# A two-block model on one core: the second layer's modulation sums moved from the first block into the first recurrent layer, and six fixed experts in a new order of units

## The reference

```python
merged = jax.nn.sigmoid(ga) * y_a + jax.nn.sigmoid(gb) * y_b
x = x + merged @ w_out[l]
h2 = rms_norm(x, norm2_g[l]).reshape(B * T, D)
# top-1 group of 4, top-2 of its 8 experts: 256 tokens, 2 of 32 experts each
for e in range(N_EXPERTS):
    he = jax.nn.silu(h @ w_gate[e]) * (h @ w_up[e])
    y = y + comb[:, e:e + 1] * (he @ w_down[e])
x = x + y
```

```python
c_act = jax.nn.silu(c)
for l in range(DEPTH_2):
    mod = c_act @ w_ada[l] + b_ada[l]          # (1, 3072), w_ada[l] is 1024 x 3072
    shift, scale, gate = jnp.split(mod, 3, axis=-1)
    h = rms_norm_2(x, norm_g[l]) * (1.0 + scale[:, None, :]) + shift[:, None, :]
    u = h @ w_in[l]
    rg_x, rg_z, ml_x, ml_o, ml_z = jnp.split(u, split_pts, axis=-1)
    ... # y_rg: conv of 4 taps, gates, linear recurrence; y_ml: conv, q, k, v, chunked mLSTM
    y = jnp.concatenate([y_rg, y_ml], axis=-1) @ w_out[l]
    x = x + gate[:, None, :] * y
```

## Time and profile before

| | |
|---|---|
| median of 3 runs | 1090.07 us (1086.15 to 1094.87) |
| the profiled execution | 1092.46 us, span 1090.70 us |
| mean granted TensorE clock | 0.952 |
| busy: PE, DVE, ACT, POOL | 990.6, 418.7, 262.2, 166.7 us |
| TensorE's first pass on an expert, last mix | 302.31; ends 524.8 us |
| layer 0: from the first transpose | 541.61 us |
| layer 1: from the first transpose | 812.09 us |
| read from memory | 224.76 MB, 207 GB/s over the span |

### The profile page before, as it was taken

The page is one execution under the profiler, slowest core; times in us unless marked ns, Lnnn a source line. Parts: engine busy times, 40 slices in busy tenths (PEclk is TensorE's granted clock), DMA queues, the critical chain, the costliest instruction groups (busy, mean ns, idle before and its releaser), DMA issues.

```text
span 1090.7 us, 14384 instructions
## 1 busy us (share of the span) xinstructions
PE 990.6 (91%) x5605; PEld 784.5 (72%) x5605; DVE 418.7 (38%) x922; ACT 262.2 (24%) x597; POOL 166.7 (15%) x147
## 2 busy tenths in 40 slices
PE   4979999999899999776499999999989999999995
PEld 4857877788766555443288887887868888788784
DVE  2149762247613131111552470634235246163411
ACT  2122222201311212100308143223011714323200
POOL 5477997601100000000000000000000000000000
PEclk9888999989899999888799999999999999999998
DMA  8774866449999999999534443323433444332301
GB/s 237 251 252 130 244 215 209 155 149 302 398 376 420 421 420 421 420 422 407 166 116 155 154 154 118 116 78 100 132 116 125 146 154 154 117 117 78 116 1 58
DMA packets 138448, 226.79 MB, mean 208 GB/s; under 512 B 6329, under 2 KB 124434, under 8 KB 126090
## 3 DMA queue, kind: packets, MB, share of 16 engines
q1 hardware_dynamic: 136632, 221.41, 56.9%
q0 software_dynamic: 1600, 4.35, 1.6%
q10 hardware_dynamic: 146, 0.08, 0.0%
HBM read 224.76 MB, written 1.06 MB: 207 GB/s over the span
## 4 chain that ended last, share of the span: by engine, by line
PE 77%; SPq 7%; DVE 6%; DMA 4%; ACT 3%; issue 2%; DVEq 0%; ACTq 0%; POOLq 0%
PE bank L456 32%; PE bank L1039 10%; SPq L1076 7%; PE bank L902 5%; PE bank L767 4%; PE bank L673 3%; PE bank L917 3%; DMA s<-in_w_up 3%; PE bank L743 2%; PE bank L803 2%; PE bank L782 2%; PE bank L439 1%; DMA ring<-in_w_in 1%; PE bank L566 1%; PE bank L932 1%
## 5 line engine op out<-in xcount | busy, mean ns | idle before, releaser
L456 PE MATMUL bank<-hT,ring 128*128 128x256 f32 x1488 | 332.9, 383 | 0.0
L456 PEld LDWEIGHTS bank<-hT,ring 128*128 128x128 f32 x1488 | 282.3, 192 | 44.5 <-issue 7.1
L1039 PE MATMUL bank<-ring,s 128*128 128x256 f32 x512 | 114.4, 386 | 3.3 <-DVE s L1923 3.3
L1039 PEld LDWEIGHTS bank<-ring,s 128*128 128x128 f32 x512 | 99.2, 194 | 17.8 <-DVE s L1923 3.8
L2063 POOL DMA_DIRECT2D gateB<-in_final_g x1 | 0.6, 594 | 545.9 <-DVE x L1931 545.9
L767 PE MATMUL bank<-s,z 128*32 128x256 f32 (+1 forms) x448 | 64.6, 432 | 9.0 <-DMA s<-in_w_up 5.8
L1720 DVE SCALAR_TENSOR_TENSOR z<-z,bank 128x256 f32<-128x256 f32 x10 | 4.2, 421 | 162.2 <-ACT z L1276 161.1
L2016 POOL TENSOR_TENSOR ring<-ring,csil 128x2048 f32<-128x2048 f32 x17 | 61.3, 3604 | 18.1 <-PE bank L482 17.2
L902 PE MATMUL bank<-ring,hT 128*128 128x256 f32 x256 | 56.1, 380 | 0.0
L902 PEld LDWEIGHTS bank<-ring,hT 128*128 128x128 f32 x256 | 48.5, 190 | 7.4 <-issue 0.9
L767 PEld LDWEIGHTS bank<-s,z 128*32 128x32 f32 (+1 forms) x448 | 35.2, 133 | 19.4 <-issue 15.3
(11 more groups left out here) (387 smaller groups left out, 1431.5 us busy)
## 6 DMA issues: line engine op xcount, KB each, us to landing
ring<-in_w_in SPq DMA_DIRECT2D x56, 1024.0 KB, 5.1
ring<-in_w_ada SPq DMA_DIRECT2D x24, 1024.0 KB, 6.0
ring<-in_w_out SPq DMA_DIRECT2D x20, 1024.0 KB, 5.0
s<-in_w_down SPq DMA_DIRECT2D x18, 1024.0 KB, 20.0
s<-in_w_gate SPq DMA_DIRECT2D x15, 1024.0 KB, 25.4
s<-in_w_up SPq DMA_DIRECT2D x13, 1024.0 KB, 21.5
ring<-in_w_up SPq DMA_DIRECT2D x12, 1024.0 KB, 20.8
ring<-in_w_gate SPq DMA_DIRECT2D x10, 1024.0 KB, 21.9
```

The lines of the kernel that those rows point to most:

```text
L456: mm = pe.matmul(b[:, 0:T], w[:, (k0 + kb) * CW + m * P:(k0 + kb) * CW + (m + 1) * P], rhs[:, kb, :], start=(kb == 0), stop=(kb == nk - 1))
L1039: mm = pe.matmul(xo[j, tt][:, 0:CW], yT[:, kb, tt * P:(tt + 1) * P], w[:, kb, :], start=(kh == 0 and kb == 0), stop=(kh == 1 and kb == KB ...
```

## The change

1. The 12 chunks of layer 1's modulation leave the first block. They stand between layer 0's weight chunks: one after each of rx and rz, after every second mx, and after each of the first two chunks of the output gate. GpSimd sums all 24; VectorE's sums are gone. The second twelve go to a new tile `adasum1` with two buffers, so GpSimd starts chunk n when TensorE has used n - 2. GpSimd starts on them behind its pads, which wait for the norm at the head of layer 0. In the first block, eight chunks stand as before and four beside ga.
2. Six experts are fixed (0 to 5), so 18 parts can be loaded before the routing is known, as many as there are slots. Two places are left for heavy ones.
3. The sequence is SLSLSLHLLL. The parts of the three fixed pairs are loaded first, then all others in order of use; each part beyond the 18th takes the slot of the part used 18 places before it.
4. The product that sorts the keys (`reorder_out`) stands between the gates and the ups of unit 0 instead of behind both, and VectorE's picks for unit 1 stand behind its result.
5. The branch without slots walks over units instead of pairs, with four buffers of activations.

```diff
-FIXED, HEAVY, LIGHT_SLOTS = 4, 4, 32
-SEQUENCE = "SSLHLLHLLL"
+FIXED, HEAVY, LIGHT_SLOTS = 6, 2, 32
+SEQUENCE = "SLSLSLHLLL"
...
-ADA_CHUNKS = LAYERS * 3 * D // CW
+ADA_CHUNKS = 3 * D // CW
 ADA_LAG = 2
-ADA_POOL = 17
...
+        adasum1 = sb("adasum1", [P, 2, CW])
...
         for c in (C_GA, C_GB):
             for j in range(4):
                 add((full, cols_of(w_in, c + j * CW)))
-                add_ada()
+                if c == C_GA:
+                    add_ada()
...
+        def addt_ada():
+
+            l, j = ada_left.pop(0)
+            tail_ada.append(len(tail))
+            addt((full, cols_of(a["w_ada_2"][l], j * CW)))
         for l in range(LAYERS):
             wi2 = a["w_in_2"][l]
             for j in range(4):
                 addt((full, cols_of(wi2, j * CW)))
+                if l == 0:
+                    addt_ada()
...
+        expert_use = [(j, c) for _, j0, G in UNITS for c in range(3) for j in range(j0, j0 + G)]
+        expert_order = [(j, c) for j, c in expert_use if LOAD_RANKS[j] < FIXED] + \
+            [(j, c) for j, c in expert_use if LOAD_RANKS[j] >= FIXED]
+        expert_chunk = {jc: E0 + m for m, jc in enumerate(expert_order)}
+        slot = [n % RING for n in range(NB1)] + moe_slots
+        for m in range(NM, 3 * EXPERTS):
+            before = expert_chunk[expert_use[m - NM]]
+            assert before < E0 + m
+            slot.append(slot[before])
+        slot += [(NB1 + t) % RING for t in range(len(tail))]
...
+                    if (u, c) == (0, 0):
+                        reorder_out()
...
                         for m in range(2):
                             projT(w, m, hT, A, f"{name}{l}{2 * j + m}")
                         used()
+                        if l == 0 and (name == "rz" or j % 2):
+                            ada_job()
...
-                out_gate(0)
-                out_gate(1)
+                for j in range(2):
+                    out_gate(j)
+                    if l == 0:
+                        ada_job()
...
                 headT(wq, lambda k: mc[:, k, :], "mq")
                 used()
+                if l == 0:
+                    for _ in range(ADA_LAG):
+                        ada_sum()
...
+                    c = ada_at[n]
+                    g.wait_ge(slot_full[slot[c]], fill_value[c])
+                    back = 3 if n < ADA_CHUNKS else 2
+                    if n >= back and not ADA_CHUNKS <= n < ADA_CHUNKS + back:
+                        g.wait_ge(A.done, A.upto(f"ada{n - back}"))
...
             step(g.memset(vaug[:, :, :, MLD:VW], 1.0), S["pads_ready"])
+            ada_sums(ADA_CHUNKS)
             g.wait_ge(S["layer_done"], LAYERS)
```

More of the change, by code:

```diff
@@ L339, in build @@
         ada_chunks = []
-        ada_left = [(l, j) for l in range(LAYERS) for j in range(3 * D // CW)]
+        ada_left = [(l, j) for l in range(LAYERS) for j in range(ADA_CHUNKS)]
         def add_ada(n=1):
@@ L389, in build @@
                 addt((full, cols_of(a["w_out_2"][l][kh * D:(kh + 1) * D, :], j * CW)))
+        assert not ada_left
         E0 = NB1
@@ L680, in _ @@
                     route(j - 1, (0, 1), (A.free, A.upto(f"xT{j - 1}1")))
-                for _ in range((1, 1, 2, 0)[j]):
-                    ada_job()
             turn_x(A, 3, (0,))
@@ L686, in _ @@
             route(3, (1,), (C.free, C.upto("xT31")))
-            for _ in range(ADA_LAG):
-                ada_job()
             pe.wait_ge(S["routed"], 1)
@@ L859, in _ @@
                 pe.wait_ge(S["xgT_ready"], 4)
-                for p in range(PAIRS):
-                    pair_all(p)
+                for u in range(NU):
+                    unit_all(u)
             for j, c in expert_order:
@@ L1101, in _ @@
                         sp.wait_ge(*sem_value)
-                if j >= FIXED and j not in ids:
+                if LOAD_RANKS[j] >= FIXED and j not in ids:
                     if not ids:
@@ L1227, in _ @@
                     step(f(oaT[o:o + 64, g // 2, :], b[o:o + 64, 0:T], ACT.Copy), A.free)
-            for _ in range(4):
-                ada_job()
             load_root_table()
@@ L1321, in _ @@
                     out_copy(rxv[:, m, PAD:PAD + T], T)
+                    if l == 0 and m % 2:
+                        ada_job()
                 for h in range(KB):
@@ L1342, in _ @@
                     out_copy(mxv[:, m, PAD:PAD + T], T)
+                    if l == 0 and m in (3, 7):
+                        ada_job()
                 act.wait_ge(S["rg_root_wanted"], l + 1)
@@ L1559, in _ @@
                 step(tten(gmT[:, g, :], b[:, 0:T], guT[:, g, :], ALU.mult), B.free)
-            ada = {"n": ADA_POOL}
-            def ada_sums(count):
-                for n in range(ada["n"], ada["n"] + count):
-                    c = ada_chunks[n]
-                    v.wait_ge(slot_full[c % RING], fill_value[c])
-                    v.wait_ge(A.done, A.upto(f"ada{n - 3}"))
-                    w, dst = full(ring[c % RING]), adasum[:, n % 3, :]
-                    step(tsc(dst, w[:, 0, :], csil[:, 0:1], None, ALU.mult))
-                    for kb in range(1, KB):
-                        ins = stt(dst, w[:, kb, :], csil[:, kb:kb + 1], dst, ALU.mult, ALU.add)
-                        step(ins, S["ada_summed_v"]) if kb == KB - 1 else step(ins)
-                ada["n"] += count
             v.wait_ge(S["small_loaded"], 16 * 5)
@@ L2009, in ada_sums @@
                 for n in range(ada["n"], ada["n"] + count):
-                    c = ada_chunks[n]
-                    g.wait_ge(slot_full[c % RING], fill_value[c])
-                    if n >= 3:
-                        g.wait_ge(A.done, A.upto(f"ada{n - 3}"))
-                    w = full(ring[c % RING])
+                    c = ada_at[n]
[3 more added lines that the diff above has]
+                        g.wait_ge(A.done, A.upto(f"ada{n - back}"))
+                    w = full(slots_of[slot[c]])
                     step(g.tensor_tensor(w, w, csil[:, :].unsqueeze(2).broadcast_to([P, KB, CW]), ALU.mult))
```

157 lines of the change are left out of this document (80 added, 77 removed).

## The result

| | before | after |
|---|---|---|
| median | 1089.48 us (1086.15 to 1094.87, 4 runs) | 1127.45 us (1124.22 to 1129.36, 4 runs) |
| span of the profiled execution | 1090.7 us | 1125.3 us |
| mean granted TensorE clock | 0.952 | 0.943 |
| busy: PE, DVE, ACT, POOL | 990.6, 418.7, 262.2, 166.7 us | 997.0, 454.2, 262.5, 234.1 us |

The account below looks back on a forecast made before the run. It took transfers to bound the experts' stage and TensorE the first block and layers. Saving 3.4 us before layer 0 and losing 29.7 in it gave +26.3: 1116 us, own range 1108 to 1124, 8 in 10 1100 to 1129.

Parts of the forecast that it names:

- rival 3: Layer 0 costs its upper bound of 38 us and starving takes all the prefetch's gain: 1128; chance 0.12.
- (b): Layer 0's first convolution: VectorE held by GpSimd, gate products 5 us later, then a 1.4 us bank wait.
- (c): Layer 0's second convolution, held by GpSimd: output gate's fourth tile waits 6.1 us, chunk 24's sum 2.5 before k.
- the clock: TensorE's granted clock in layer 0, partly at its lower level behind the waits: 1.4 us more.
- What bounds the kernel: Whole kernel: experts' stage bound by transfers, first block and the two layers by TensorE.
- First block and experts' stage: Before layer 0: earlier order, 18 parts loaded ahead, then unit 1 starved of slots; 3.4 us less in all.
- (a): Layer 0's head: VectorE's chain held at each GpSimd instruction, so TensorE starts 9.0 us late.
- block 7 ends at about 670: Second convolution's last block, delayed by GpSimd: end at about 670 us where it was 638.9.
- The weighed rule: Skill's rule: GpSimd contends only with two-port or two-SBUF-input VectorE instructions; (b) and (c) would be about 2 us less.
- Rival 1: Layer 0: VectorE not slowed where it matters, layer 0 costs only 7.1 us, total 1094; chance 0.10.
- Rival 2: Experts' stage: prefetch pays, DMA never starves, gain 17 us instead of 3.4, total 1103; chance 0.12.
- Rival 4: Experts' routing: the change does not do what it says, all goes through the dense branch, over 1200; chance 0.01.

Follow-up runs that it names:

- late_pairs: Changed kernel with sequence SSLSLLHLLL, GpSimd waiting for the normed x and, after two of layer 1's chunks, for the first convolution; 1113.64 us.
- late_head: Changed kernel with one more wait: GpSimd starts layer 1's chunks only when the normed x is ready; 1116.38 us.
- split_sums: Changed kernel with layer 1's chunks summed in eight GpSimd instructions of at most 512 columns instead of four; 1112.91 us.
- fine_sums: Changed kernel with layer 1's chunks summed in pieces of 256 columns, 15 GpSimd instructions a chunk; 1130.24 us.

## Why the prediction was right or wrong

The measured 1127.45 lies outside the forecast's own range (1108 to 1124) and inside the range of 8 in 10 only because that one reaches to rival 3, so the hit is a narrow one. On the profiled execution 1118.8 was said and 1127.0 measured, 8.2 us more. Of these, layer 0 up to k has 8.1 (37.8 for 29.7), nearly all in (b), (c) and the clock.

**What bounds the kernel** held: the experts' stage on transfers, layer 0 on TensorE until VectorE is late. One row was misread: the 27.36 us of the earlier trace rows are a w_up load from issue to landing, and TensorE's wait for it, at 505.87, is 6.16.

**First block and experts' stage: -3.4 said, -4.8 measured.** The course was as told: unit 0's gates at 299.56 (said 298.9), the fourth up in unit 1 at 329.85 (said 329.2), the pass ending at 335.53 (said 335.5). Only the wait is 7.58 and not 9. The prediction's own end times, 518.1 and 521.5 from starts 3.4 us apart, leave nothing for the prefetch; the traces show 2.75 for the start and 2.05 for the stage itself, so the near hit is in part luck. The starving behind the filled slots was the right reason for the small gain: the 277 GB/s are the same in late_pairs with another order. Not foreseen: 1.15 us between the last mix and L893. VectorE's last sum ends 0.8 us behind the mix in both kernels (520.76, 525.55); what grew is its idle time behind that, 5.22 us for 4.07, for which the profile names no releaser. The cause is open.

**(a) The head: 9.0 said, 9.1 measured.** The chain of holds, worked out instruction by instruction from four rows of the first block, gave TensorE's delay to 0.1 us, and late_head confirms the cause.

**(b) The first convolution: 5.0 + 0.7 said, 7.5 measured.** The blocks end at one per chunk, as told. Not in the sum: the gate products behind the wait (4.32 us, at 590.05) run at TensorE's lower clock (0.54 granted over 590.05 to 593.68), 1.22 us for two matmuls that take 0.67 elsewhere. Up to rz they take 593.68 - 590.05 = 3.6 us, where the kernel before had 2.0: 1.6 of the 1.8 us that were missing. The bank wait behind it is 1.29, said 1.4.

**(c) The output gate: 6.1 said, 10.92 measured. This is the term that was mis-sized.** The step that failed is "block 7 ends at about 670". That is in the times of before. The changed kernel comes to layer 0 3.65 us sooner (L893 at 527.52 for 531.17), so it stands for 666.4 in its trace, and the block ended at 674.30, 7.9 us later. TensorE came to the fourth tile 3.1 us later than in the sum (664.35 for 671.0 - 6.1 - 3.65 = 661.25), and the difference, 4.8, is what the wait has too much. I had said that three blocks (2, 6, 7) cross GpSimd's work, and let GpSimd run at 8.26 us a chunk. In the trace the wide instructions of the gates (L1845 to L1847, L1850) are held, 2.29 becoming 4.29 in the first and 3.95 in the last; the convolution so starts at 629.35, behind them, and not at 612.74 as before; and GpSimd is held in turn, with its instruction of 1.27 at 3.19 and that of 3.60 at 5.53, so that a chunk there takes up to 12 us, and its later chunks lie over more of the convolution. Five blocks of eight were held, and four of them took over 8 us. The 1.4 us for the clock was too little as well: the gate products lost 1.6, the pass behind this wait 1.7, and the k projection's pass, behind the end of the sum, another 1.7. The wait for chunk 24's sum was right, 2.19 for 2.5.

**The weighed rule.** The prediction took the convolution's first instruction, "one input at 0.41 us for 256 columns", for one that the rule would let go free. It was held, to 3.68 us at 573.05 and 3.58 at 581.60, so the trace was on the side of the sum. The earlier trace rows had spoken for it already: L1555, a TENSOR_SCALAR between SBUF tiles, went from 0.35 to 3.27. But the rule was not refuted, I had read the row wrongly. 256 columns in 0.41 and 1024 in 0.75 are 0.34 / 768 = 0.44 ns a column, where SCALAR_TENSOR_TENSOR with 0.51 for 256 and 2.29 for 2048 is at 0.99. And once let go, it ends 0.16 us behind GpSimd (576.73 against 576.57), the SCALAR_TENSOR_TENSOR behind it 0.29 (579.30 against 579.01), both of 256 columns. So a TENSOR_SCALAR of this kind does about two columns for the other's one, which shows in the slope and is hidden in the duration. The Trainium skill (VectorE: DVE Perf Modes, section "Mode 2×_2P — use both read ports for one tensor") says that this mode takes both read ports and is how an fp32 tensor_scalar comes to twice the rate; the slope agrees, and if it is in that mode, the rule quoted in the prediction holds it. That it is in the mode, and that the mode is what makes it subject to the hold, is argued here and no run isolates it.

**The rivals.** Rival 1 (VectorE not slowed) is ruled out by the rows of the head. Rival 2 (the prefetch pays, 17 us) is ruled out by the stage, 2.05 us shorter, and by the 277 GB/s. Rival 3 named 1128 and the result is near it, but not for its reasons in full: it has the stage end as before, and it ended 4.8 us sooner, 2.05 of them from the prefetch and the order; what it had right is that the scans are held too (L1861, 691 to 1493 ns) and that the clock costs more. Rival 4 does not apply.

## What to carry to other kernels

Before work is put on an idle engine, ask what it shares with the busy ones, and work the meeting out instruction by instruction: here the length of one GpSimd instruction, and not GpSimd's load, set what VectorE lost, until pieces grew so small that TensorE waited for the sums (1127 with up to 2048 columns, 1113 with 512, 1130 with 256). Where an engine has a short chain that others wait for, keep the other one out of it: one wait on GpSimd gave back 11 us of 38. And filling all slots ahead gains only what the slots' release can follow up; six parts more in memory, with the new order, were worth 2 us of 15. A stage that ends sooner may only have begun sooner; the kernel with the other half of the change alone tells.

## What the runs showed of the hardware

- The hold is mutual, and whichever started first goes on to its end. Timeline of GpSimd, with VectorE's 2048 columns wide instructions of L1845 to L1847 running from 605.15 to 615.45:

```profile
604.94 2.35 POOL L2035 TENSOR_TENSOR ring<-ring 128x1024 f32<-128x1024 f32 x1
607.38 3.19 POOL L2036 TENSOR_TENSOR ring<-ring 128x512 f32<-128x512 f32 x1
610.65 2.65 POOL L2037 TENSOR_TENSOR adasum<-ring 128x256 f32<-128x256 f32 x1
613.38 5.53 POOL L2034 TENSOR_TENSOR ring<-ring,csil 128x2048 f32<-128x2048 f32 x1
```

L1845 (605.15, 4.29 us) is held until 607.29 and then takes 2.15. GpSimd's next is held until 609.44 and then takes 1.13. They alternate, one instruction each. The Trainium skill (SBUF — State Buffer, section "Who interferes with whom") says the same of the port pair that the two share, that whoever issues first has it for the whole instruction and the other "fully blocks"; the trace agrees: once let go, L1845 takes 2.15 where it takes 2.29 alone, and GpSimd's next 1.13 where it takes 1.27.
- Not held, in the midst of GpSimd's instructions: RECIPROCAL on two columns (0.17), and TENSOR_SCALAR from PSUM (L1492 from 547.89 on, the first two of eight beside GpSimd, 4.60 us for all; they take 0.54 each in both kernels). Held: TENSOR_SCALAR between SBUF tiles even on two columns (0.17 to 2.20), TENSOR_TENSOR, SCALAR_TENSOR_TENSOR and TENSOR_TENSOR_SCAN.
- On GpSimd a product of 2048 columns takes 3.60 us alone, four of 512 columns take 4.40 (split_sums) and eight of 256 columns 5.45 (fine_sums), each with its gaps: 0.26 us for every cut.
